# A transformer block on one Trainium2 core: the mixer's split weights kept in DRAM and reloaded, and the first expert's weights fetched during routing

## The reference

```
h = LN0([meta, x])
q,k,v,cb,cc,ch,ga,gc = split(h @ w_in)              # one input projection
mix = (sig(ga)*(attn(q,k,v) @ w_attn_out) + sig(gc)*((cb*conv3(cc*ch)) @ w_conv_out)) @ w_o
h = LN1(alpha*h + mix)
g = argmax group of 4; e1,e2 = top 2 of its 8 experts  # 32 experts, hidden width 512
out = LN2(alpha*h + sum_e weight_e * (silu(h @ w_gate[e]) * (h @ w_up[e])) @ w_down[e])[16:]
```

## Time and profile before

| | us |
|---|---|
| median of 3 runs | 4327.14 (4320.51 to 4341.16) |
| the profiled execution | 4333.28 |
| its span, first to last instruction | 4331.5 |
| TensorE busy in it | 4171.0 (96%) |
| VectorE, ScalarE, GpSimd busy | 2518.7, 1773.0, 1094.6 |
| mean granted clock of TensorE | 0.988 |

### The profile page before, as it was taken

How to read it: one execution, slowest core, us unless ns; L and a number is a source line. 1 busy time by engine, 2 the same in 40 slices (tenths; PEclk the granted TensorE clock), 3 DMA queues, 4 the chain that set the end, 5 groups by cost and what they waited for, 6 DMA issues and landing times. The chain is left out here.

```text
span 4331.5 us, 62892 instructions
## 1 busy us (share of the span) xinstructions
PE 4171.0 (96%) x20252; PEld 3428.8 (79%) x20253; DVE 2518.7 (58%) x3263; ACT 1773.0 (41%) x2950; POOL 1094.6 (25%) x1117
## 2 busy tenths in 40 slices
PE   7999999999999999999999999499999999999997
PEld 7887887887887888888888887388788888778886
DVE  5555555555555655645645645777666666765664
ACT  2422422422422422422422422466555555654553
POOL 4022032022022021121121121134333333333333
PEclk9999999999999999999999999799999999999998
DMA  6333333333333333333332332187666666765562
GB/s 171 85 107 103 93 102 98 99 104 97 102 104 89 107 106 85 107 104 89 111 102 80 117 102 78 54 289 248 246 199 198 206 199 234 251 203 198 194 204 90
DMA packets 569472, 601.49 MB, mean 139 GB/s; under 512 B 104080, under 2 KB 426640, under 8 KB 569248
## 3 DMA queue, kind: packets, MB, share of 16 engines
q1 hardware_dynamic: 521152, 476.88, 35.5%
q0 software_dynamic: 48096, 121.71, 8.4%
HBM read 527.15 MB, written 124.78 MB: 151 GB/s over the span
## 5 line engine op out<-in xcount | busy, mean ns | idle before, releaser
L826 PE MATMUL bank<-hT_hi,w_hi 128*128 128x512 f32 x2176 | 864.8, 397 | 30.1 <-DVE w_lo L658 21.3
L658 DVE TENSOR_TENSOR w_lo<-raw,w_hi 128x1024 fp32r<-128x1024 f32 x400 | 597.3, 1493 | 485.5 <-ACT w_hi L517 484.4
L827 PE MATMUL bank<-hT_lo,w_hi 128*128 128x512 f32 x2176 | 850.6, 391 | 2.4 <-issue 2.4
L828 PE MATMUL bank<-hT_hi,w_lo 128*128 128x512 f32 x2176 | 849.2, 390 | 0.0
L1565 PE MATMUL e_bank<-e_w_hi,e_xT_hi 128*128 128x512 f32 x1312 | 521.9, 398 | 14.2 <-DVE e_xT_lo L1488 12.4
L826 PEld LDWEIGHTS bank<-hT_hi,w_hi 128*128 128x128 f32 x2176 | 408.9, 188 | 140.4 <-DVE w_lo L658 32.6
L1567 PE MATMUL e_bank<-e_w_hi,e_xT_lo 128*128 128x512 f32 x1312 | 514.3, 392 | 0.0
L1566 PE MATMUL e_bank<-e_w_lo,e_xT_hi 128*128 128x512 f32 x1312 | 513.4, 391 | 0.0
L1493 DVE TENSOR_TENSOR e_w_lo<-e_raw,e_w_hi 128x1024 fp32r<-128x1024 f32 x384 | 444.4, 1219 | 117.7 <-ACT e_w_hi L1441 110.8
L828 PEld LDWEIGHTS bank<-hT_hi,w_lo 128*128 128x128 f32 x2176 | 408.9, 188 | 87.4
L827 PEld LDWEIGHTS bank<-hT_lo,w_hi 128*128 128x128 f32 x2176 | 409.3, 188 | 86.6 <-issue 5.4
(11 more groups left out here) (277 smaller groups left out, 7173.3 us busy)
## 6 DMA issues: line engine op xcount, KB each, us to landing
raw<-in_w_in_dram SPq DMA_DIRECT2D x251, 512.0 KB, 3.9
e_raw<-in_w_exp_gate_dram SPq DMA_DIRECT2D x128, 512.0 KB
e_raw<-in_w_exp_up_dram SPq DMA_DIRECT2D x128, 512.0 KB
e_raw<-in_w_exp_down_dram SPq DMA_DIRECT2D x128, 512.0 KB
h_rows<-h_rows SPq DMA_DIRECT2D x72, 512.0 KB, 3.5
raw<-in_w_o_dram SPq DMA_DIRECT2D x64, 512.0 KB, 3.8
raw<-in_w_in_dram SPq DMA_DIRECT2D x64, 256.0 KB, 3.7
raw<-in_w_attn_out_dram SPq DMA_DIRECT2D x64, 256.0 KB, 2.8
```

The costliest lines, as they stand in the source:

```text
L658: v.tensor_tensor(w_lo[:, s % 2, :], raw[:, s % RAW, :], w_hi[:, s % 2, :].bitcast(FP32), ALU.subtract).then_inc(lo_ready, 1)
L826: pe.matmul(out, hi, x_hi, start=first, stop=False)
L827: pe.matmul(out, hi, x_lo, start=False, stop=False)
L828: return pe.matmul(out, lo, x_hi, start=False, stop=last)
```

## The change

The mixer's first block is written out by itself and loads `raw` and splits as before, now two strips ahead (`split_hi(s + 2)`, `split_lo(s + 2)`), with three buffers `raw` and four slots of 1 MB that each hold both parts of a strip (three of them used in this block). After a strip is split, SyncE stores both parts in a DRAM tensor of 50 MB. The other seven blocks are a loop in which SyncE loads the split strips, 1 MB each, three strips ahead, when strip s is done; ScalarE and VectorE split nothing there. The attention steps stand one strip later (`ATT0`). Layer norm on GpSimd keeps only 1/deviation; VectorE makes the rest in two operations of two tensors each. The next block's x is loaded at strips 21 to 24. At routing, SyncE loads all 12 chunks of expert 0, ScalarE makes the high parts of 8, GpSimd clears the down chunks; the experts stage begins with eight low parts on VectorE and the rows' split after them.

```diff
-    RAW = 5
+    RAW, META_RAW = 3, 5
+    SLOTS = 4
+    ahead = RAW
+    slot_of = list(range(SLOTS)) * 5 + [0, 1, 2] + list(range(SLOTS)) * 6 + [0, 1, 2]
+    ATT0 = CONV0 + 1
...
-        X_AT = {MIX0 + 8 + i: i for i in range(TILES)}
+        X_AT = {MIX0 + 3 + i: i for i in range(TILES)}
...
+                def store_split(s):
+
+                    sp.wait_ge(lo_ready, s + 1)
+                    sp.dma_start(split_d[s], slots[first_slot(s)][:, :, :].rearrange("p h d -> p (h d)").bitcast(FP32))\
+                      .then_inc(w_out[first_slot(s)], 16)
...
+                def block_of_loads(b, first):
                     for s in range(N):
-                        load(s + 1, b)
+                        if first:
+                            store_split(s)
+                        if first and s + ahead < N:
+                            load_raw(s + ahead)
+                        else:
+                            hold(sp, strip_done, b * N + s + 3)
...
+                            load_split((s + ahead) % N, b + (s + ahead) // N)
...
-                    v.tensor_scalar(rows[:, i1, :], rows[:, i1, :], moments[:, i1, 0:1], rstd[:, i1, 0:1],
-                                    ALU.subtract, ALU.mult).then_inc(ln_normed, 1)
+                    gain, shift = (g1, b1) if rows is h else (g0, b0)
+                    v.scalar_tensor_tensor(out=rows[:, i1, :], in0=rows[:, i1, :], scalar=moments[:, i1, 0:1],
+                                           in1=gain[:, :], op0=ALU.subtract, op1=ALU.mult).then_inc(ln_normed, 1)
+                    v.wait_ge(ln_normed, n + 1)
+                    v.scalar_tensor_tensor(out=rows[:, i1, :], in0=rows[:, i1, :], scalar=rstd[:, i1, 0:1],
+                                           in1=shift[:, :], op0=ALU.mult, op1=ALU.add).then_inc(ln_done, 1)
...
-                        split_lo(s + 1)
+                        if first and s + 2 < N:
+                            split_lo(s + 2)
...
-                        pe.wait_ge(lo_ready, b * N + RAW + s + 1)
+                        if first:
+                            pe.wait_ge(lo_ready, s + 1)
+                            w_of = slots[first_slot(s)]
+                        else:
+                            pe.wait_ge(w_in[slot_of[s]], w_uses(s, b))
+                            w_of = slots[slot_of[s]]
...
+                block_of_strips(0, True)
+                with nc.Fori(1, BLOCKS, engines=bass.OrderedEngineSet([pe.engine]), hint_back_edge=True) as b:
+                    block_of_strips(b, False)
...
+                for w in (weights["w_hi"], weights["w_lo"]):
+                    po.memset(w[:, weights["early"]:, :].bitcast(FP32), 0.0)
...
-                for c in range(2 * GC, CH):
-                    v.memset(w_hi[:, c, :].bitcast(FP32), 0.0)
-                    v.memset(w_lo[:, c, :].bitcast(FP32), 0.0).then_inc(down_lo, 1)
+                v.sem_inc(down_lo, DC)
...
                 for c in range(2 * GC):
-                    if c == GC:
-                        evacuate(0)
                     split_lo(0, c)
+                evacuate(0)
```

More of the change, by code:

```diff
@@ L180, in place @@
             return placed
+        at = [weights]
+        slots = [place(at, f"w_slot{i}", [P, 2, D], F32R) for i in range(SLOTS)]
+        raw = place([weights + 4 * 6 * D], "raw", [P, RAW, D])
+        meta_raw = place([weights + 4 * 4 * D], "meta_raw", [P, META_RAW, D])
         at = [shared]
@@ L402, in mixer @@
         h1_out = [sem(f"h1_out{i}") for i in range(TILES)]
+        w_in = [sem(f"w_in{i}") for i in range(SLOTS)]
+        w_out = [sem(f"w_out{i}") for i in range(RAW)]
         hi_ready = sem("hi_ready")
@@ L439, in mixer, with raw_uses, w_uses @@
         LNS = 2 * TILES
[L441 to L446 removed]
+        def raw_uses(s):
+            return sum(16 * len(strip_dmas(*strips[q], raw[:, 0, :])) for q in range(s % RAW, s + 1, RAW))
+        def w_uses(s, b):
+            slot = slot_of[s]
+            return 16 * ((b - 1) * slot_of.count(slot) + slot_of[0:s + 1].count(slot))
         with nc.Block() as block:
@@ L473, in _ @@
                             sp.dma_start(xs[:, i1, :], x[bass.ds(nxt * TOK + i1 * P, P), :]).then_inc(x_in[i1], 16)
+                for s in range(ahead):
+                    load_raw(s)
+                block_of_loads(0, True)
+                with sp.Fori(1, BLOCKS) as b:
+                    block_of_loads(b, False)
+                for s in range(ahead):
+                    sp.wait_ge(w_in[slot_of[s]], w_uses(s, BLOCKS))
                 for i1 in range(TILES):
@@ L602, in _ @@
                              .then_inc(hx_hi, 1)
+                for s in range(2):
+                    split_hi(s)
+                block_of_strips(0, True)
+                with nc.Fori(1, BLOCKS, engines=bass.OrderedEngineSet([a.engine]), hint_back_edge=True) as b:
+                    block_of_strips(b, False)
                 for i in range(TILES):
@@ L802, in _ @@
                     assert steps[0] == DVE_STEPS
+                for s in range(2):
+                    split_lo(s)
+                block_of_strips(0, True)
+                with nc.Fori(1, BLOCKS, engines=bass.OrderedEngineSet([v.engine]), hint_back_edge=True) as b:
+                    block_of_strips(b, False)
                 v.wait_ge(wo_taken, BLOCKS * 2 * TILES + 1)
@@ L1061, in route, with _ @@
         with nc.Block() as block:
+            @block.sync
+            def _(sp):
+                for c in range(weights["chunks"]):
+                    load_expert_chunk(sp, t, weights, 0, c)
+                for dst, row in ((weights["gain"], t["ln2_g"]), (weights["shift"], t["ln2_b"])):
+                    sp.dma_start(dst[:, :], row.unsqueeze(0).to_broadcast([P, row.shape[0]]))\
+                      .then_inc(weights["consts_in"], 16)
             @block.gpsimd
```

197 lines of the change are left out of this document (97 added, 100 removed).

## The result

The changed kernel takes 4292.41 us (median of 4 runs, 4289.16 to 4294.11), the kernel before on the same chip 4330.08 (4 runs, 4320.51 to 4341.16): a ratio of 0.9911, with a 95% interval of 0.9894 to 0.9929. The forecast was 4296.7, range 4284 to 4325, and faster by over 0.5% with a chance of 0.73.

The account below looks back on a forecast made before the run. The prediction took TensorE's own instructions to bound the mixer, leaving only its waits to win: 21.3 + 5.5 + 3.6 = 30.4 us off the 4327.1 us median gives 4296.7 us, range 4284 to 4325.

Parts of the forecast that it names:

- Step 6: Mixer loop's back edges: one fewer of seven and a branch hint, counted as 0, other end -2.4 us.
- Step 1: Mixer blocks 2 to 8: low and high parts removed, TensorE's 20 waits for low parts go, -21.3 us.
- Step 2: Mixer, all 8 blocks: attention one strip later removes TensorE's wait for q's evacuation, -5.5 us.
- Step 3: Mixer's layer norm: gain and bias from GpSimd to VectorE, whose load in those strips falls, cost 0.
- Step 4: Mixer's 1 MB loads of split strips: landing 5.2 us, 11.2 at worst beside stores, against 11.0 available; cost 0.
- Rival (a): Mixer: split-strip loads land later than 11.0 us, making the kernel slower, 4344 or up to 4496 us; chance 0.10.
- Step 5: Mixer's first block: storing 1 MB and loading 512 KB a strip stays hidden, cost 0, at most 4 us.
- Step 7: Routing: expert 0's loads, high parts and GpSimd clearings fit into idle time, cost 0.
- Rival (b): Routing: GpSimd's clearings hold up VectorE by up to 7.0 us, 4303.7; chance 0.12 together with (c).
- Step 8: Start of the experts: eight clearings leave VectorE's queue, so the first expert product comes sooner, -3.6 us.
- (c): First block's stores cost 4 us and experts start no sooner (3.6), 4304.3 us; chance 0.12 together with Rival (b).
- (d): Mixer: removed waits turn into others of the same length, only the experts' start gains, 4323.5 us; chance 0.08.

## Why the prediction came out right, and where it was off

- **What bounds the kernel** was right: TensorE's own instructions bound the mixer, and only its waits could be won. It is the steps' sizes that were off, -40.2 us in the traces for -30.4: the mixer gave 14.7 more than forecast and routing 4.6 less. The medians' -37.7 meets a kernel before that is 3.0 us slower than the median that the sum started from. So that 4292.4 lies 4.3 from the forecast is in part luck. The 11.8, 25.1 and 7.4 us of steps 6, 1 and 2 below, less 2.1 for the late load and 0.9 for slower first products, make up the mixer's 41.5 within 0.2.
- **Step 6, back edges, 0, other end -2.4**: the largest mis-sized term. The seven edges of the kernel before cost 11.8 us, and in the changed kernel all of it is gone. The step took them at the 2.4 listed, and took a hint for no gain. It also had no term for the cost of the hint behind the loop, where routing's first part lost 5.1 us, 3.8 of it one issue gap.
- **Step 1, the splits removed, -21.3**: right in mechanism. Of the 20 waits four (2.6 us) stood at the edges; the other 16 cost 22.0 for the 18.7 listed, and 2.4 us behind the probabilities and 0.7 elsewhere in the blocks weren't on the list. That is 25.1 us. The term took the list at face value, and what a wait costs is 0.18 to 0.27 more than is listed.
- **Step 2, attention a strip later, -5.5**: right, measured -7.4 (0.95 a block for 0.69 listed). It holds only with step 1 done; alone it makes the kernel slower.
- **Step 3, gain and bias on VectorE, 0**: right in the blocks of the changed kernel, and behind the loop it spares 2.8 us that no step had. The sentence that VectorE's load in those strips falls was true only since the low parts are gone. Alone the edit costs 25 us.
- **Step 4, the loads, 0**: right, no wait for a load behind the third strip of the second block. Landing is 4.8 us (5.2 taken). The burst at strips 4 to 7 reached 7.7 to 8.6 us for the estimated 11.2, and the bound of 11.0 was wrong too: attention's strips give 13 to 14. The loads of x are a second tight place, which the step doesn't have. Rival (a) is refuted with a margin: neither half the time nor twice the bytes makes the kernel slower than before.
- **Step 5, the first block's stores, 0 to 4**: the traffic was hidden, as said, though 2.5 MB a strip are 477 GB/s by the megabyte of step 4 and not 455, and the backlog 1.3 us a strip. The loss of 2.1 us in the second block came from another cause, the order in which SyncE issues stores and waits.
- **Step 7, routing, 0**: right. Rival (b) is refuted as it was put: clearings on GpSimd leave VectorE's chain at 16.3 us to the hundredth. Beside GpSimd's low parts, which read, the chain does stretch: in that run from the logits to the ranks it took 22.6. The rule of the Trainium skill (SBUF — State Buffer, Who interferes with whom), contention of two-input VectorE operations with GpSimd's reads and not with its writes, is what both traces show.
- **Step 8, start of the experts, -3.6**: right, -4.1 from the counted ranks to the product, 3.7 with the step undone. Routing as a whole is longer by 1.0 for the 5.1 us of step 6.
- Rivals (c) and (d) didn't occur. The fear of (d), that VectorE's layer norm makes new waits, is just what happens when that part is done without the splits' removal.

## What to carry to other kernels

Where TensorE is the bound, read its list of waits as a lower bound: add about a quarter of a microsecond for each, and lay the starts of its products in both traces side by side, since the list leaves short pauses out and more than half of what the back edges cost. A part of a change that is worth nothing or does harm alone may be harmless beside the part that empties a queue, so parts are priced in the order in which they can hold. For a prefetch compare landing with the strips it really has ahead, at the place of the burst, and look in the issuing queue for a wait that stands before a transfer whose data are long ready.

## What the runs showed of the hardware that I had not expected

- A wait of TensorE between matmuls of 512 columns costs 0.27 us beyond the listed idle time, 0.26 ahead of the transposes of v, and 0.18 behind the 208-column products (1.26 listed at 437.78).
- A hinted back edge costs TensorE nothing that the trace shows (1.6 to 2.1 us without, 1.2 to 1.4 of it in one gap), and the loop's exit has a gap of 3.8 us, in the code behind it, that is there only with the hint.
- Two-input VectorE operations wait for the end of the GpSimd operation under way, if that reads two tensors: 0.19 becomes 1.9 to 2.3 us at 32 columns; beside clearings they keep their time (r_masked, 1024 columns, 1.22 us from 2687.64 in the changed kernel, within the clearings of 2685.14 to 2692.1).
- 1 MB loads beside as many bytes copied in DRAM: 347 GB/s over a block at a DMA share of 0.89, with median landings of 4.8 to 8.2 us outside the bursts.
